# Two transformer-like blocks on one core: order of the opening and mixing of block 1, place of the rope tables and of the weight loads

## What is computed

```python
def rmsnorm(x, g): ...                       # x * rsqrt(mean(x*x) + eps) * g, over the features
h = rmsnorm(x, norm_g)
proj = jnp.einsum('bsd,dc->bsc', h, w_in)
# branch B, "mixing"
uv = jax.nn.gelu(buv)
u, vb = uv[..., :B_WIDTH], uv[..., B_WIDTH:]
vb = layernorm(vb, sgu_ln_g, sgu_ln_b).reshape(B, S // B_CHUNK, B_CHUNK, B_GROUPS, B_GROUP_DIM)
mixed = jnp.einsum('gts,bnsgc->bntgc', w_causal, vb) + sgu_b.T[None, None, :, :, None]
yb = u * mixed.reshape(B, S, B_WIDTH) * jax.nn.silu(bz)
# branches A and C
qa, ka = partial_rope(aq, positions), partial_rope(ak, positions)   # needs cos and sin of the positions
lam = exp(sum(lam_q1 * lam_k1)) - exp(sum(lam_q2 * lam_k2)) + lam_init
```

## Time and profile before

| | |
|---|---|
| median of 3 runs | 4046.81 us (4042.68 to 4050.09) |
| the profiled execution | 4042.67 us |
| its span, first to last instruction | 4040.9 us |
| mean granted TensorE clock | 0.964 |
| TensorE (PE) busy | 3743.9 us, 93% |
| VectorE (DVE) busy | 1718.9 us, 43% |
| ScalarE (ACT) busy | 1265.5 us, 31% |
| GpSimd (POOL) busy | 1091.6 us, 27% |
| chain that ended last | PE 70%, DVE 14%, ACT 7%, issue 5%, DMA 2%, POOL 2% |
| moved by DMA | 243.91 MB, mean 60 GB/s |

### The profile page before, as it was taken

One profiled execution on the slowest core, in us unless ns is written; L12 is line 12 of the kernel. 1 busy time (PEld: TensorE's weight loads), 2 busy tenths in 40 slices (PEclk: granted clock), 3 DMA queues, 4 the chain that ended last, 5 costly groups with the idle time before them and its releaser, 6 DMA issues.

```text
span 4040.9 us, 51127 instructions
## 1 busy us (share of the span) xinstructions
PE 3743.9 (93%) x20820; PEld 3311.2 (82%) x20820; DVE 1718.9 (43%) x3136; ACT 1265.5 (31%) x2868; POOL 1091.6 (27%) x806
## 2 busy tenths in 40 slices
PE   6999998999999899999899999968988998898898
PEld 5787777888887788777778888858988998898898
DVE  6624554433325552455443332554334334333333
ACT  3212443034331211244313333122245422134541
POOL 2533222321113362322231221326310023530002
PEclk9999999999999999999999999979989999998999
DMA  3111110401114212111130112322100031110012
GB/s 113 37 68 63 35 50 32 147 31 42 42 40 176 87 42 78 47 40 44 42 141 29 42 40 79 130 83 65 43 26 19 20 108 56 60 52 13 14 41 95
DMA packets 85195, 243.91 MB, mean 60 GB/s; under 512 B 10720, under 2 KB 25312, under 8 KB 84960
## 3 DMA queue, kind: packets, MB, share of 16 engines
q1 hardware_dynamic: 84960, 240.64, 17.4%
HBM read 190.07 MB, written 50.53 MB: 60 GB/s over the span
## 4 chain that ended last, share of the span: by engine, by line
PE 70%; DVE 14%; ACT 7%; issue 5%; DMA 2%; POOL 2%; SPq 1%; DVEq 0%; POOLq 0%; ACTq 0%
PE pj L1212 27%; PE pS L1212 21%; PE po L1420 4%; PE po L1311 4%; PE pS L1400 3%; PE pS L1402 2%; DVE tmp L2030 1%; PE pS L1282 1%; DVE KK L2042 1%; PE pS L1283 1%; PE pt L1298 1%; DVE tmp L2033 1%; ACT PT L1612 1%; PE pj L1386 1%; DVE tmp L2027 1%
## 5 line engine op out<-in xcount | busy, mean ns | idle before, releaser
L2471 POOL TENSOR_SCALAR Whi<-stage 128x1024 fp32r<-128x1024 f32 (+4 forms) x272 | 277.8, 1021 | 2138.9 <-DMA stage<-wstream 1328.4
L1212 PE MATMUL pj<-Hhi,Whi 128*128 128x512 f32 x1648 | 657.5, 399 | 8.3 <-DVE Hlo L1901 3.3
L1212 PE MATMUL pj<-Hhi,Wlo 128*128 128x512 f32 x1648 | 645.5, 392 | 0.0
L1212 PE MATMUL pj<-Hlo,Whi 128*128 128x512 f32 x1648 | 645.0, 391 | 0.0
L2473 POOL TENSOR_TENSOR Wlo<-stage,Whi 128x1024 fp32r<-128x1024 f32 (+4 forms) x272 | 621.9, 2287 | 22.7
L1212 PEld LDWEIGHTS pj<-Hhi,Whi 128*128 128x128 f32 x1648 | 311.6, 189 | 76.3 <-ACT PT L1612 6.6
L1212 PEld LDWEIGHTS pj<-Hhi,Wlo 128*128 128x128 f32 x1648 | 311.0, 189 | 66.8
L1212 PEld LDWEIGHTS pj<-Hlo,Whi 128*128 128x128 f32 x1648 | 311.6, 189 | 61.4
L1212 PE MATMUL pS<-Hhi,Whi 128*128 128x512 f32 x784 | 312.7, 399 | 12.2 <-DVE Hlo L1901 5.1
L1212 PE MATMUL pS<-Hlo,Whi 128*128 128x512 f32 x784 | 310.0, 395 | 0.0
L1212 PE MATMUL pS<-Hhi,Wlo 128*128 128x512 f32 x784 | 309.5, 395 | 0.0
(11 more groups left out here) (389 smaller groups left out, 7735.8 us busy)
## 6 DMA issues: line engine op xcount, KB each, us to landing
stage<-wstream SPq DMA_DIRECT2D x228, 512.0 KB, 4.3
merged<-Mb SPq DMA_DIRECT2D x32, 512.0 KB, 2.9
Mb<-merged SPq DMA_DIRECT2D x32, 512.0 KB, 5.1
gates<-tmp SPq DMA_DIRECT2D x48, 256.0 KB, 2.2
TH<-gates SPq DMA_DIRECT2D x24, 512.0 KB, 6.1
xres<-X SPq DMA_DIRECT2D x16, 520.0 KB, 5.7
xr<-xres SPq DMA_DIRECT2D x16, 520.0 KB, 4.6
X<-xT SPq DMA_DIRECT2D x16, 256.0 KB, 6.8
```

The source lines that it names most:

```text
L1212: x = pe.e.matmul(ps, w[a][:, v.koff + k * P:v.koff + k * P + P], moving(v.of, b, k, v.t0, v.n), start=k == 0 and i == 0, stop=k == v.K - ...
L2471: pool.e.tensor_scalar(upper, stage, 1.0, 0.0, ALU.mult, ALU.add).then_inc(*pool.tick("whi", c))
```

## The change

1. **First norm ahead of the second half's squares.** In `first_block` only the first half is squared ahead of its root. In `norm1` of layer 1 come the norm steps k=0 and 1, then squares 0 to 3 of the second half, step 2, squares 4 and 5, step 3, squares 6 and 7, the second half's root, and steps 4 to 7. On TensorE the second half's sum moves behind k=3 of the group and its spread behind k=7 (layer 2 keeps 0 and 3).
2. **First splits.** Weight 0 is split on GpSimd ahead of the first root, weight 1 behind it, weight 2 behind that.
3. **Loads by last use.** `upto`, `ahead` and the `first_weights` units of `norm2` are gone. From c=3 on, DMA and split of weight c stand at the unit behind the one that uses weight c-3 last.
4. **Column tiles alternate.** The second-half tiles of v0, v1, v2 are a group too, k outermost.
5. **Layer norm in two.** A new unit `lnlow` holds `vbhi` and `vblo`. The order is: one filler; then for each n `ln`, filler, `lnlow`, filler, `lnmix`. There are 16 fillers, as before.
6. **Tables.** They leave `mixing`; in layer 1 two groups stand behind each of the 16 merge tiles of branch B, and the rest behind the last. Their tiles move to a place that is free in the merge, with four work tiles in place of five, and `yb` no longer waits for them.

```diff
 in memory():
-    o = y0
-    m.posi = at("posi", o, [P, S], I32)
-    m.ang = [at(f"ang{i}", o + 4096 * (i + 1), [P, S]) for i in range(5)]
+    m.ang = [at(f"ang{i}", s1 + 20480 + 4096 * i, [P, S]) for i in range(4)]
+    m.posi = at("posi", s1 + 24576, [P, S], I32)
...
 in Order.__init__():
-        loaded = 0
-        for u, upto in self.upto:
-            last = min(upto, len(self.weights) - 1)
-            u["loads"] = range(loaded, last + 1)
-            loaded = max(loaded, last + 1)
+        at = 0
+        for c in range(len(self.weights)):
+            at = max(at, self.first[c].id if c < NR else self.used_at[c - NR] + 1)
+            self.units[at].setdefault("loads", []).append(c)
+            self.units[self.split[c].id if c < NR else at].setdefault("splits", []).append(c)
...
 in first_block():
-        for i, (t0, n) in enumerate(TC1):
-            for k in range(8):
-                self.square("1", k, i, t0, n, ("x_in", i, k))
-            if i == 0:
-                sums = self.rstd("1", [self.accs[0]], D, 0)
+        for k in range(8):
+            self.square("1", k, 0, *TC1[0], ("x_in", 0, k))
+        self.split.append(self.put("first_split"))
+        sums = self.rstd("1", [self.accs[0]], D, 0)
+        self.split.append(self.put("first_split"))
...
 in norm1():
-        self.upto.append((self.put("first_weights"), len(self.weights) + NR - 1))
+        if l == 0:
+            self.first.append(self.put("first_weights"))
+            self.split.append(self.first[2])
         self.norm(of, 0, range(2), rs, self.x_ready[0], self.h_free[0])
+        if l == 0:
+            for ks, k in (range(4), 2), (range(4, 6), 3), (range(6, 8), None):
+                for q in ks:
+                    self.square("1", q, 1, *TC1[1], ("x_in", 1, q))
+                if k:
+                    self.norm(of, 0, [k], rs, self.x_ready[0], self.h_free[0])
         other = self.rstd("1", [self.accs[1]], D, 1, within=True)
-        self.norm(of, 0, range(2, 8), rs, self.x_ready[0], self.h_free[0])
+        self.norm(of, 0, range(2 if l else 4, 8), rs, self.x_ready[0], self.h_free[0])
...
-        self.inside = {0: [other], 3: [rs]}
+        self.inside = {0: [other], 3: [rs]} if l else {3: [other], 7: [rs]}
...
 in mixing():
-        self.together([v[0][0], v[1][0], v[2][0]], self.inside)
-        for u in [v[0][1], v[1][1], v[2][1]] + v[3]:
-            self.add(u)
-            self.aside()
-            self.aside()
-            self.aside()
+        self.together([v[j][0] for j in range(3)], self.inside)
+        self.together([v[j][1] for j in range(3)], {})
+        self.run(v[3])
...
+        self.fill()
         for n in range(8):
             u = self.put("ln", ...)
             self.pt_free = ("ln_out", u.id)
-            self.bt_free[4 + n % 2] = ("lo", u.id)
-            for _ in range(2):
-                self.fill()
-                self.aside()
-            x = self.put("lnmix", l=l, n=n, c=u.c, ln=u.id, po_free=self.po_free, wc_ready=wc_ready)
+            self.fill()
+            y = self.put("lnlow", ln=u.id, w=w, vb_free=vb_free)
+            self.bt_free[w] = ("lo", y.id)
+            self.fill()
+            x = self.put("lnmix", l=l, n=n, c=u.c, low=y.id, po_free=self.po_free, wc_ready=wc_ready)
...
-        while self.aside():
-            pass
-        self.tables_ready = [("tab_act", "sin", 1), ("tab", "sign"), ("tab", "gains")]
-        self.y_free = self.y_free + self.tables_ready
...
 in merge():
+        self.table_steps = self.table_groups() if first and l == 0 else iter(())
...  behind each merge tile:
+                self.aside()
+                self.aside()
...
 in vector_program():
         TS(w[:, :], m.pt[:, :], st[:, b + 6:b + 7], st[:, b + 9:b + 10], ALU.subtract, ALU.mult).then_inc(
             *dve.tick("ln_out", u.id))
+
+    def lnlow(u):
         dve.wait_ge(("hi", u.id))
         dve.wait_ge(u.vb_free)
-        lo(m.vb[1][:, :], w[:, :], m.vb[0][:, :], u.id)
+        lo(m.vb[1][:, :], m.bt[u.w][:, :], m.vb[0][:, :], u.id)
...
 in gpsimd_program():
-        for c in u.loads or ():
+        for c in u.splits or ():
             load(c)
```

More of the change, by code:

```diff
@@ L303, in __init__ @@
     def __init__(self):
-        self.units, self.weights, self.upto = [], [], []
+        self.units, self.weights, self.first, self.split, self.used_at = [], [], [], [], {}
         self.bank, self.banks, self.bank_free = 0, WIDE, [None] * 6
@@ L328, in add @@
         if u.opens:
-            u.box["c"] = self.weight(u, u.key, u.ahead)
+            u.box["c"] = self.weight(u.key)
         if u.box is not None:
             u["c"] = u.box["c"]
+            if u.ends:
+                self.used_at[u.c] = u.id
         if u.banked:
@@ L361, in take, with weight @@
         return b, self.bank_free[b]
-    def weight(self, u, key, ahead=None):
+    def weight(self, key):
         self.weights.append(key)
-        i = len(self.weights) - 1
-        self.upto.append((u, i + (NR - 1 if ahead is None else ahead)))
-        return i
+        return len(self.weights) - 1
     def phase(self):
@@ L434, in first_block @@
         self.put("load_x", i=0)
-        self.upto.append((self.put("first_weights"), 1))
+        self.first += [self.put("first_weights")] * 2
         self.put("load_x", i=1)
@@ L446, in first_block @@
         self.restok = []
-        self.tables_ready = []
         for l in range(DEPTH):
@@ L529, in gate, with column @@
             return sets
-        def column(make, name, j, toks, emptied, ahead=None):
+        def column(make, name, j, toks, emptied):
             box = {}
             sets = gate(j) if make == "gate_u" else gelu(toks, j)
-            return self.in1(make, l, COL["b" + name] + j * P, j=j, box=box, sets=sets, emptied=emptied, ahead=ahead)
-        v = [column("gelu_v", "v", j, vtok, "gelu", 2 - j if j < 3 else None) for j in range(4)]
-        self.together([v[0][0], v[1][0], v[2][0]], self.inside)
-        for u in [v[0][1], v[1][1], v[2][1]] + v[3]:
-            self.add(u)
-            self.aside()
-            self.aside()
-            self.aside()
+            return self.in1(make, l, COL["b" + name] + j * P, j=j, box=box, sets=sets, emptied=emptied)
+        v = [column("gelu_v", "v", j, vtok, "gelu") for j in range(4)]
+        self.together([v[j][0] for j in range(3)], self.inside)
+        self.together([v[j][1] for j in range(3)], {})
+        self.run(v[3])
         for j in range(4):
@@ L609, in merge @@
                 self.mtok[d] = self.mb_stored[d % 4] = ("mb_out", y.id)
+        while self.aside():
+            pass
         if final:
@@ L867, in fourier_pool @@
         self.put("small_in", l=l)
-        f = [self.in2("f_copy", key("f", i), x=i, box={}, emptied="f_copy", ahead=NR - 1 - i) for i in range(2)]
-        p = [self.in2("p_copy", key("p", i), x=i, box={}, emptied="p_copy", ahead=i * (NR - 1)) for i in range(2)]
+        f = [self.in2("f_copy", key("f", i), x=i, box={}, emptied="f_copy") for i in range(2)]
+        p = [self.in2("p_copy", key("p", i), x=i, box={}, emptied="p_copy") for i in range(2)]
         self.together([f[0][0], f[1][0], p[0][0]], self.inside)
@@ L894, in fourier_pool @@
                                  lts=((0, 1, 2), (3, 4))[piece], free=ps_free[2 * part:2 * part + 2])
-                    u["c"] = self.weight(u, u.dkey)
+                    u["c"] = self.weight(u.dkey)
+                    self.used_at[u.c] = u.id
             u = self.put("unfold", kc=kc, k0=k0, n=n, even=("dft", u.id - 2), odd=("dft", u.id), osb_free=osb_free,
@@ L1254, in lnmix @@
     def lnmix(u):
-        pe.wait_ge(("lo", u.ln))
+        pe.wait_ge(("lo", u.low))
         pe.wait_ge(u.wc_ready)
@@ L1582, in mix_in @@
         hi(m.wc[0][:, :, :], m.bt[4][:, :].rearrange("p (g t) -> p g t", g=4), "wc", u.l)
-    def ln(u):
-        act.wait_ge(("shifted", u.id))
+    def lnlow(u):
+        act.wait_ge(("shifted", u.ln))
         act.wait_ge(u.vb_free)
@@ L1915, in table @@
     def table(u):
-        a, k, r, ks, posf = m.ang
+        a, k, r, ks = m.ang
+        posf = r
         for op in u.ops:
@@ L1923, in table @@
                 dve.wait_ge(("const_in",))
-                dve.wait_ge(("ones",))
+                phase_met(u)
                 x = dve.e.tensor_copy(posf[:, :], m.posi[:, :])
@@ L2448, in vector_program @@
     parts = {"phase": phase, "start": start, "clear": clear, "square": square, "sums": sums, "norm": norm, "table": table, "proj": proj,
-             "mix_in": mix_in, "ln": ln, "lnmix": lnmix, "yb": yb, "merge_end": merge_end, "soft": soft, "values": values,
+             "mix_in": mix_in, "ln": ln, "lnlow": lnlow, "lnmix": lnmix, "yb": yb, "merge_end": merge_end, "soft": soft, "values": values,
              "finish": finish, "between": between, "small_in": small_in, "gmix": gmix, "fold": fold, "amix": amix,
```

12 lines of the change are left out of this document (6 added, 6 removed).

## The result

The changed kernel takes 4103.62 us, the median of 4 runs (4101.53 to 4104.78); the kernel before, measured beside it, 4045.84 us. The ratio is 1.0142, with a 95% interval of 1.0124 to 1.0159: some 58 us slower. I had predicted 4038.8, with a range up to 4053. The profiled execution took 4102.85 us.

What follows compares the result with a forecast made beforehand. TensorE's idle time and lower clock were taken to bound the kernel. Terms 13+6+4+2-15-1-1 = 8 us off the median 4046.81 gave 4038.8 us, range 4022 to 4053.

Steps and rivals of the forecast that it cites:

- the other splits in attention A: Attention A: ten more splits a layer ahead of a root, 1.4 us late, covered by a tile: -1 us.
- the seams: Attention A, three places a layer: a split beside the `KK` subtractions costs 2.5 us each, -15 us in all.
- Slower: Rival, attention A: splits ahead of roots hold ScalarE, 20 steps at 1.4 us uncovered, 4067 us; chance 0.12.
- The sign that I had named: Middle of attention A: TensorE waiting for `PT` there would show the prediction wrong; no size given.
- My upper bound of 28: Attention A, ten more splits a layer ahead of roots: 20 steps at 1.4 us uncovered, at most -28 us.
- if the seams stay at 4.5: Sign of being wrong, attention A: waits expected to be 7 us at six places staying at 4.5.
- Layer 1's opening: Block 1's start: first matmul 2.7 us earlier, new waits of 2.2 and 3.0; I take 3 us later.
- The four gains: Block 1: layer 1 +13 us, layer 2 +6; block 2: opening +4, layer 2 +2.
- The tile: Extra column tile ahead of first `ln`: 5.6 and 2.3 us in layer 1, fills 6.0 of wait in layer 2.
- The tables: Beside the first merge: 27 groups two by two behind merge tiles, -1 us, bounds 0 and -4.
- Seams free: Rival, attention A: the splits hide in the attention seams, time 4023.8 us; chance 0.24.
- Mixing not won: Rival, first mixing: VectorE stays behind TensorE, layer 1's 13 goes to 0 or 3, 4049 to 4052 us; chance 0.17.

Runs made afterwards that it cites:

- the three weights: Changed kernel, all weights loaded and split at the opening of c-2 except 90, 178 and 226, which stay behind the last use of c-3: 4022.69 us, repeated 4015.37.
- the slow version: The changed kernel itself, all its parts in, against the kernel before: 4103.62 us, ratio 1.0142.
- the fast one: Changed kernel with attention A's splits back at the opening of c-2, transfers left at the changed place: 4044.33 us, 0.9998.

## Why the prediction was wrong

**The step that failed** is the term of the sum for the other splits in attention A, -1: "Ten more splits a layer (3.5 us each) move ahead of a root ... so it comes 1.4 us late; the tile of 5.6 that follows covers it: -1". It measured 44 us: 58 in attention A (1.0142 against 0.9998) less 14 for the seams. I found the right place and twenty roots there, and had the mechanism as my rival "Slower"; its price was wrong, and with it the chance of 0.12. The sign that I had named, that TensorE waits for `PT` in the middle of attention A, came true: 12.2 us instead of 1.3. Three things were in it.

- I priced the split by its two operations, 3.5 us. It also waits for its transfer, and the rule moves that too: it is issued behind the gate's store, 5 us ahead of its data. With the transfers out of the way the 58 become 24; of those 14 are the seams, which leaves some 10 us for 1.5 us a root. That is what my 1.4 late costs, ten times the 1 that I gave for it; the cover of a tile did not hold everywhere even then. The transfer was the other 34.
- What tells of it was in the trace before. GpSimd waited 1328.4 us for transfers ahead of `Whi` in 89 waits, and it was harmless, since behind those waits nothing was due. After the move there was.
- My upper bound of 28 took 1.4 for each of the 20 as the most. A bound for an operation placed ahead of another must hold what it waits for, not just what it lasts.

**The second step that failed** is one that is not in the prediction's text. I priced the new rule at the openings and in attention A, and everywhere else at nothing. It cost some 20 us there: the sliding sums of block 2 (10.5 instead of 5.7, twice), the output projections' opening ("issue", 4.6 and 5.4 instead of 2.3 and 2.2), and the rest at places that no run took apart, the latent tiles among them.

**What held.** The seams: -15, measured 14. But not as I described them: I expected TensorE's waits of 4.5 for `tmp` to become 7, and named "if the seams stay at 4.5" as a sign that I am wrong. That row is still 39.4 us in 26 waits, the longest 4.5, and yet the seams cost what I said. The split meets the first of the two `KK` pairs of a seam, and TensorE pays where it waits for that pair, at `pS`: 0.7 at most before, up to 3.8 after. Layer 1's opening: first matmul at 25.96 (I had 26.7), then waits of 2.30 and 3.05 (2.2 and 3.0), `Wlo` 2.75 (3.8). The row that stands where the wait of 11.3 was:

```profile
93.74 0.65 PE L1257 MATMUL pt<-ident,VT 128*128 128x128 f32 x4 [0.70 <-DVE VT L2005]
```

I had 94.1. That is close in part by luck: I let eight gelus end near 93, which by my own lengths end near 95, and `ln` waits for the seventh only. The last `lnmix` waits 2.01 in both layers (2), but the clock falls behind it (0.55 in 191:196), which I had left out. The four gains, each by the start of the same matmul in both traces: layer 1, 12.7 by the end of its mixing and 10.4 by the merge (13); layer 2, 5.4 (6); block 2's opening, 5.0 (4), where `Fx` takes the place of the 9.57 with 4.2; its second layer, 0.3 (2), since the wait for `H2lo` grew from 2.7 to 4.8 as that for `Wlo` went. One trace is a loose measure of this: in the seven traces whose programs are the same up to attention A, it begins between 356.3 and 361.3. The tile was over-priced: 8 for both layers rather than 14. The tables cost nothing that the trace shows. In all, the rest of the change without its loading rule is worth 17 us, and with the three weights 20 to 22, where my steps gave 24.

**The sum, by what was measured:** 22 gained; 14 lost at the seams, 44 on the roots in attention A and 21 elsewhere: 57 slower, where 58 was measured. These are differences of ratios, each good to some 6 to 8 us, so that they meet within 1 is luck. The rival "Seams free" is excluded by the 14, "Mixing not won" by the 12.7.

The Trainium skill (SBUF — State Buffer, Who interferes with whom) says that a VectorE instruction with two SBUF inputs contends with a GpSimd instruction that reads SBUF, and it calls the pair of ports that the two engines share an exclusive lock. The trace agrees. Here is the first seam of the changed kernel, where each of the two `KK` subtractions takes 0.69 alone. The first, begun ahead of `Wlo`, takes 0.74; the second, begun beside it at 443.19, takes 2.72 and ends at 445.9, half a microsecond behind `Wlo`:

```profile
442.42 3.49 DVE L2049 TENSOR_TENSOR KK<-tmp,KK 64x512 fp32r<-64x512 f32 x2 [0.70 <-ACT KK L1563]
...
442.71 2.65 POOL L2482 TENSOR_TENSOR Wlo<-stage,Whi 128x1024 fp32r<-128x1024 f32 x1
```

The sentence of the Trainium skill that I weighed the seams by (Advanced Engine Details and Errata, VectorE Performance Modes) names only "2p Vector instructions" and would have made them free; the 14 us that six seams cost go against that reading.

## What to carry to other kernels

An engine that works in order has one queue for heavy work with slack and small work without. Before you move a heavy item earlier, list what it will stand ahead of, and take as its length everything up to its end, the waits for its inputs among them, above all if the same edit makes those inputs later. A long idle time "waiting for a transfer" is free only as long as nothing behind it is due. List also what it will run beside: an operation of another engine can be stretched by it without waiting for it. And a rule for all loads has to be priced at each kind of place it touches, not only where it was meant to help.

## What the runs showed of the hardware

A VectorE subtraction of two tensors in SBUF that takes 0.69 us alone took 2.72 at the seams with GpSimd's `Wlo` (2.65) beside it, and a pair of subtractions at the output projections 3.43 instead of 1.47. And one place in a program is enough: the same split, 3.5 us long, is free behind a root of 0.55 us and costs up to 8.6 us of ScalarE's time ahead of it, its wait for its own data included.

The six seam splits gave 5 us when taken out of the slow version and cost 14 when added to the fast one. The intervals do not quite part the two, but the traces say why the first can be too small: with the roots still late, VectorE stayed behind TensorE at the seams.
